# Building the expert gates of a routed layer: one-hot marks for 16 tokens in four products, and routing lookups merged over the heads

## The reference, cut to what matters

```python
q = (xb @ wq).reshape(PEER_BLOCK, PEER_HEADS, 2, PEER_HALF)
s = jnp.einsum('thpd,hpkd->thpk', q, sub_keys)             # 8 heads, 2 halves, 128 keys
s_top, i_top = lax.top_k(s, PEER_TOPK)                     # 16 of 128, twice
cand_s = s_top[:, :, 0, :, None] + s_top[:, :, 1, None, :] # pairs
cand_i = i_top[:, :, 0, :, None] * 128 + i_top[:, :, 1, None, :]
best_s, best_pos = lax.top_k(cand_s, PEER_TOPK)            # 16 of the pairs
experts = jnp.take_along_axis(cand_i, best_pos, axis=-1)
g = jax.nn.softmax(best_s, axis=-1)
act = gelu(einsum('thkd,td->thk', expert_u[experts], xb))
return einsum('thk,thkd->td', g * act, expert_v[experts])
```

## Time and profile before

| what | us |
|---|---|
| median of three runs | 2895.91 |
| profiled execution | 2900.16 |
| its span | 2898.3 |
| PE busy | 2657.9 (92%) |
| PEld busy | 2140.2 (74%) |
| DVE busy | 1856.9 (64%) |
| ACT busy | 949.5 (33%) |
| POOL busy | 1643.7 (57%) |

### The profile page before, as it was taken

How to read it: one execution, slowest core, us unless ns; L and a number is a source line. 1 busy time by engine, 2 the same in 40 slices (tenths; PEclk the granted TensorE clock), 3 DMA queues, 4 the chain that set the end, 5 groups by cost and what they waited for, 6 DMA issues and landing times.

```text
span 2898.3 us, 36976 instructions
## 1 busy us (share of the span) xinstructions
PE 2657.9 (92%) x13468; PEld 2140.2 (74%) x13468; DVE 1856.9 (64%) x3298; ACT 949.5 (33%) x1656; POOL 1643.7 (57%) x964
## 2 busy tenths in 40 slices
PE   7999999999899999999899999918777889999998
PEld 6888787678767788788677888816565667888886
DVE  6432398744664444200365079999999966888886
ACT  2001312833474101111242144314343444444443
POOL 4665457965403566646645557616455556666673
PEclk9999999999999999999999999959898999999998
DMA  4223122122342322322213245514454558888883
GB/s 157 87 87 121 58 88 94 31 66 77 110 146 109 116 92 112 109 88 101 98 41 111 92 175 217 217 44 182 170 217 200 217 217 306 290 289 289 289 289 131
DMA packets 139988, 429.93 MB, mean 148 GB/s; under 512 B 8800, under 2 KB 79584, under 8 KB 116704
## 3 DMA queue, kind: packets, MB, share of 16 engines
q1 hardware_dynamic: 125376, 353.40, 33.8%
q10 hardware_dynamic: 7200, 68.68, 6.1%
q0 software_dynamic: 7296, 6.31, 0.9%
HBM read 358.10 MB, written 73.40 MB: 149 GB/s over the span
## 4 chain that ended last, share of the span: by engine, by line
PE 64%; DVE 18%; issue 8%; POOL 6%; DMA 2%; ACT 1%; DVEq 1%; SPq 0%; ACTq 0%; POOLq 0%
PE bank L1144 8%; PE bank L1145 8%; DVE work L2316 6%; PE bank L697 4%; PE bank L698 4%; PE bank L700 4%; POOL rpb_tiles L2464 3%; PE bank L958 3%; PE bank L953 3%; PE bank L954 3%; PE bank L755 3%; PE bank L727 3%; PE bank L749 3%; PE bank L728 3%; PE bank L732 3%
## 5 line engine op out<-in xcount | busy, mean ns | idle before, releaser
L2502 POOL TENSOR_TENSOR expert_parts<-ring,expert_parts 128x1024 fp32r<-128x1024 f32 x256 | 696.3, 2722 | 495.4 <-ACT expert_parts L1586 492.7
L2526 POOL CAST w_parts<-ring 128x1024 fp32r<-128x1024 f32 (+3 forms) x212 | 228.8, 1079 | 636.3 <-DMA ring<-in_wstream 153.0
L2528 POOL TENSOR_TENSOR w_parts<-ring,w_parts 128x1024 fp32r<-128x1024 f32 (+3 forms) x212 | 512.1, 2416 | 17.0
L1586 ACT ACTIVATE expert_parts<-ring 128x1024 fp32r<-128x1024 f32 x256 | 271.2, 1060 | 538.5 <-PE bank L1145 531.0
L1144 PE MATMUL bank<-h_rounded,expert_parts 128*128 128x512 f32 x1024 | 414.0, 404 | 0.7 <-ACT work L1598 0.7
L1144 PE MATMUL bank<-weighted,expert_parts 128*128 128x512 f32 x1024 | 401.9, 393 | 9.9 <-DVE weighted L2348 9.9
L1145 PE MATMUL bank<-h_rest,expert_parts 128*128 128x512 f32 x1024 | 406.1, 397 | 0.0
L1145 PE MATMUL bank<-weighted,expert_parts 128*128 128x512 f32 x1024 | 401.5, 392 | 0.0
L2316 DVE SCALAR_TENSOR_TENSOR work<-const,trig,work 128x256 f16<-128x256 f32 x512 | 346.3, 748 | 0.0
L2348 DVE SCALAR_TENSOR_TENSOR weighted<-weighted,hF 128x512 fp32r<-128x512 f32 x128 | 309.5, 2419 | 51.3 <-ACT weighted L1666 48.1
L1144 PEld LDWEIGHTS bank<-weighted,expert_parts 128*128 128x128 f32 x1024 | 194.2, 190 | 51.2 <-issue 6.0
(11 more groups left out here) (430 smaller groups left out, 5155.4 us busy)
## 6 DMA issues: line engine op xcount, KB each, us to landing
ring<-in_wstream SPq DMA_DIRECT2D x128, 2048.0 KB, 7.8
hidden<-hF ACTq DMA_DIRECT2D x32, 1024.0 KB, 4.0
gates<-work ACTq DMA_DIRECT2D x16, 2048.0 KB, 10.7
hF<-hidden SPq DMA_DIRECT2D x32, 1024.0 KB, 9.5
work<-gates SPq DMA_DIRECT2D x32, 1024.0 KB, 12.8
rpb_tiles<-in_rpb POOLq DMA_DIRECT2D x192, 16.0 KB, 2.2
work<-rpb_tiles POOLq DMA_DIRECT2D x24, 128.0 KB, 5.4
ring<-in_wstream SPq DMA_DIRECT2D x5, 512.0 KB, 4.0
```

The costliest lines, as they stand in the source:

```text
L1586: act.activation(expert_chunk(j, 0), ring_chunk(p, j), ACT.Copy, scale=1.0 - 1.0 / SPREAD)\
L2502: nc.gpsimd.tensor_tensor(expert_chunk(j, 1), ring_chunk(p, j), expert_chunk(j, 0), ALU.subtract).then_inc(made, 1)
L2526: g.tensor_copy(parts[0], source).then_inc(hi, 1)
L2528: g.tensor_tensor(parts[1], source, parts[0], ALU.subtract).then_inc(made, 1)
```

## The change

- G_A and G_B are laid out with tokens innermost: G_A as [part, number, token], G_B as [number, token], 16 tokens adjacent. A new constant tile, G_RULER, holds each number 0 to 127 sixteen times.
- A batch of marks is four instructions of 2048 16-bit elements each, all operands 16-bit: compare with the first index, compare with the second index, multiply the first marks by the gate's high part, and (in place) by its low part. The first and the third are followed by a wait for their end. The 16 instructions L2316 and the one L2323 of a batch go.
- A product's operands are now every sixteenth 16-bit number of these tiles (a step of 32 bytes). Their number, shape and order stay.
- ScalarE's three copies of the banks, and `choice_moved` with TensorE's wait for it, go. VectorE waits for the transposes and reads banks 4 to 6 itself, with four instructions of 512 elements; G_RULER is made before that wait.
- In `routing`, the eight instructions L2265 of a quarter become one of 960 elements, and the eight L2291 of a half become one of 2048.

```diff
-        G_A = area(24576, 2, GC, N_KEYS).bitcast(f16).rearrange("p b t (l r) -> p b t l r", l=2)
-        G_B = area(28672, 2, GC, N_KEYS // 2).bitcast(f16)
+        G_A = area(24576, 2, 2 * N_KEYS * GC // 2).bitcast(f16).rearrange("p b (l r t) -> p b l r t", l=2, t=GC)
+        G_B = area(28672, 2, N_KEYS * GC // 2).bitcast(f16).rearrange("p b (r t) -> p b r t", t=GC)
+        G_RULER = area(30720, N_KEYS * GC // 2).bitcast(f16).rearrange("p (r t) -> p r t", t=GC)
...
-                                mm = pe.matmul(bank[:, 4 + b, t * P:(t + 1) * P], G_B[:, j // 2, 4 * b + t, :],
-                                               G_A[:, j // 2, 4 * b + t, l, :], start=(l == 0), stop=(l == 1))
+                                mm = pe.matmul(bank[:, 4 + b, t * P:(t + 1) * P], G_B[:, j // 2, :, 4 * b + t],
+                                               G_A[:, j // 2, l, :, 4 * b + t], start=(l == 0), stop=(l == 1))
...
-                pe.wait_ge(signal("choice_moved"), 3)
...
-                for c in range(3):
-                    act.wait_ge(signal("choice_turned"), c + 1)
-                    act.activation(E_T[c], bank[:, 4 + c, :], ACT.Copy).then_inc(signal("choice_moved"), 1)
...
-                    for h in range(PEER_HEADS):
-                        ins = v.tensor_tensor(
-                            R_CAND[:, h, 16:136].rearrange("p (i j) -> p i j", i=15),
-                            sv[:, h, 0, 1:16].rearrange("p (i a) -> p i a", a=1).broadcast_to([P, 15, 8]),
-                            sv[:, h, 1, 0:8].rearrange("p (a j) -> p a j", a=1).broadcast_to([P, 15, 8]), ALU.add)
+                    ins = v.tensor_tensor(
+                        R_CAND[:, :, 16:136].rearrange("p h (i j) -> p h i j", i=15),
+                        sv[:, :, 0, 1:16].rearrange("p h (i a) -> p h i a", a=1).broadcast_to([P, PEER_HEADS, 15, 8]),
+                        sv[:, :, 1, 0:8].rearrange("p h (a j) -> p h a j", a=1).broadcast_to([P, PEER_HEADS, 15, 8]),
+                        ALU.add)
...
-                        for h in range(PEER_HEADS):
-                            ins = v.tensor_tensor(R_EQ2[:, h * 16:(h + 1) * 16, :], R_EQ[:, h * 16:(h + 1) * 16, :],
-                                                  sif[:, h, s, :].rearrange("p (a j) -> p a j", a=1)
-                                                  .broadcast_to([P, 16, 16]), ALU.mult)
-                        order(ins)
+                        order(v.tensor_tensor(R_EQ2.rearrange("p (h k) j -> p h k j", h=PEER_HEADS),
+                                              R_EQ.rearrange("p (h k) j -> p h k j", h=PEER_HEADS),
+                                              sif[:, :, s, :].rearrange("p h (a j) -> p h a j", a=1)
+                                              .broadcast_to([P, PEER_HEADS, 16, 16]), ALU.mult))
...
+                    def of(x, n):
+                        return x[:, ds(n * GC, GC)].rearrange("p (a t) -> p a t", a=1).broadcast_to([P, N_KEYS, GC])
                     for b in range(2):
                         n = 2 * m + b
                         if not first(m):
                             dve.wait_ge(gated, 4 * n - 4)
-                        for t in range(GC):
-                            ins = v.scalar_tensor_tensor(
-                                out=G_A[:, b, t], in0=cst("iota").rearrange("p (l r) -> p l r", l=1)
-                                .broadcast_to([P, 2, N_KEYS]), scalar=E_T[0][:, ds(n * GC + t, 1)],
-                                in1=G_PARTS[:, :, ds(n * GC + t, 1)].broadcast_to([P, 2, N_KEYS]),
-                                op0=ALU.is_equal, op1=ALU.mult)
-                        ins.then_inc(first_hot, 1)
-                        e = G_SECOND[:, ds(n * GC, GC)].rearrange("p (t a) -> p t a", a=1)
-                        v.tensor_tensor(G_B[:, b], G_IOTA.rearrange("p (a r) -> p a r", a=1)
-                                        .broadcast_to([P, GC, N_KEYS]), e.broadcast_to([P, GC, N_KEYS]),
-                                        ALU.is_equal).then_inc(second_hot, 1)
-                dve.wait_ge(signal("choice_moved"), 3)
...
+                        order(v.tensor_tensor(G_A[:, b, 1], G_RULER, of(G_FIRST, n), ALU.is_equal))
+                        v.tensor_tensor(G_B[:, b], G_RULER, of(G_SECOND, n), ALU.is_equal).then_inc(second_hot, 1)
+                        order(v.tensor_tensor(G_A[:, b, 0], G_A[:, b, 1], of(G_HIGH, n), ALU.mult))
+                        v.tensor_tensor(G_A[:, b, 1], G_A[:, b, 1], of(G_LOW, n), ALU.mult).then_inc(first_hot, 1)
+                order(v.tensor_copy(G_RULER, cst("iota").rearrange("p (r a) -> p r a", a=1).broadcast_to([P, N_KEYS, GC])))
+                dve.wait_ge(signal("choice_turned"), 3)
+                v.tensor_copy(G_FIRST, bank[:, 4, :])
+                v.tensor_copy(G_SECOND, bank[:, 5, :])
+                order(v.tensor_scalar(G_HIGH, bank[:, 6, :], GATE_SCALE, None, ALU.mult))
+                order(v.scalar_tensor_tensor(out=G_LOW, in0=bank[:, 6, :], scalar=GATE_SCALE, in1=G_HIGH,
+                                             op0=ALU.mult, op1=ALU.subtract))
+                order.laps(S // GC // 2, body, 4)
```

More of the change, by code:

```diff
@@ L450, in build @@
         R_E = area(6656, NT, 3, P)
-        E_T = [trig.rearrange("p a t c -> p (a t c)"), rs[:, 0, :], rs[:, 1, :]]
         U_SLOTS = N_KEYS // 4
@@ L459, in build @@
         G_STAGE = area(0, 2, N_KEYS, GT)
-        G_A = area(24576, 2, GC, N_KEYS).bitcast(f16).rearrange("p b t (l r) -> p b t l r", l=2)
-        G_B = area(28672, 2, GC, N_KEYS // 2).bitcast(f16)
[L462 to L465, removed]
+        G_A = area(24576, 2, 2 * N_KEYS * GC // 2).bitcast(f16).rearrange("p b (l r t) -> p b l r t", l=2, t=GC)
+        G_B = area(28672, 2, N_KEYS * GC // 2).bitcast(f16).rearrange("p b (r t) -> p b r t", t=GC)
+        G_RULER = area(30720, N_KEYS * GC // 2).bitcast(f16).rearrange("p (r t) -> p r t", t=GC)
+        G_HIGH, G_LOW = (area(31744 + j * S // 2, S // 2).bitcast(f16) for j in range(2))
+        G_FIRST, G_SECOND = (rs[:, j, 0:S // 2].bitcast(f16) for j in range(2))
         GATE_SCALE = 32768.0
@@ L2321, in body @@
-                        ins.then_inc(first_hot, 1)
-                        e = G_SECOND[:, ds(n * GC, GC)].rearrange("p (t a) -> p t a", a=1)
-                        v.tensor_tensor(G_B[:, b], G_IOTA.rearrange("p (a r) -> p a r", a=1)
-                                        .broadcast_to([P, GC, N_KEYS]), e.broadcast_to([P, GC, N_KEYS]),
-                                        ALU.is_equal).then_inc(second_hot, 1)
-                dve.wait_ge(signal("choice_moved"), 3)
-                v.tensor_copy(G_IOTA, cst("iota"))
```

## The result

The changed kernel takes 2989.65 us (median of four, 2986.95 to 2993.4) against 2895.07 us before: a ratio of 1.0326, 95% interval 1.0309 to 1.0344. It is 95 us slower; the forecast was 94 us faster.

What follows compares the result with a forecast made beforehand. VectorE was taken to bound routing's end and the 16 gate slots. From the profiled 2900.2 us, gate slots -56 (408.2 to 352) and routing -38 gave 2806; the runs' median lies 4.3 lower: 2802 us, range 2745 to 2884.

Steps and rivals of the forecast that it cites:

- the price of the products' operands: Gate products on TensorE: stepped operands cost twice the dense price, 109 ns a product, group 1.74 us, slot 22.0 us.
- The slow rival: Gate products stop overlapping: 219 ns each, slot 29.0 us, gate stage +57 us, total 2915 us; chance 0.11.
- its point of decision: Gate stage: the slow outcome decides from 6.97 us for a row, that is from 200 ns for a product.
- Routing: Merged instructions on VectorE ahead of the choices save 38 us (29 to 56), multiply 31.6 with six stalls; on the path in full.
- The marks: VectorE's gate batch: four packed instructions at 1.22 us, at most 9.3 us with two stalls; VectorE leaves the path.
- ScalarE's copies and the ruler: Between routing and gates: dropping the copies, VectorE reading banks itself and making the ruler cost nothing.
- The first rival's bound: Gate slots: strided operands cost nothing, VectorE and GpSimd exclude each other for 19.4 us a slot; total 2760 us; chance 0.30.

Runs made afterwards that it cites:

- The run with halves: Changed kernel with 2 tokens innermost (4-byte step on both product operands), plus GpSimd's second part of a row made by two half-size instructions: 2748.5 us, ratio 0.947.
- the 4-byte step: Changed kernel with 2 tokens innermost in place of 16, so both operands of a gate product step by 4 bytes: 2765.54 us, ratio 0.9524.

## Why the prediction was wrong

**The step that failed is the price of the products' operands.** It was named as the number that "decides most" and was left to an inference: the weight loads depend on the width of a number (98 against 188 ns), so a stepped operand costs twice. The loads are the wrong operand. The moving one sets the price, at 219 ns by itself, and the cost goes with the 16-byte pieces touched, 1.75 to 1.79 ns each. With 229 instead of 109 ns the group is 3.66 instead of 1.74 us: 64 x 1.92 = 123 us on the gate stage. The next 41 us are, all but two, the granted clock, which nothing in the forecast had: it assumed full clock once TensorE stopped waiting. Together these are 164 of the 169 us between 352 and 521; the last 5 are rows of 3.84 where 3.76 had been reckoned.

The slow rival had the price almost right (219 ns) by luck, for its reason was wrong: products still overlap (423 ns long, 241 ns from start to start); they are slow because of what they read. Its 2915 us were 75 too few, for it too left out the clock and had the larger gain in routing. It was given 0.11 although the forecast itself said that no row showed such an operand; two ends as far apart as 54 and 317 ns, on the engine that was about to become the bound, called for a range that reached its point of decision, 200 ns.

**Routing was right in kind and too large.** 38 us were forecast, 22 came (62.8 to 40.7 us of waiting). The merged multiply met GpSimd eight times out of eight, not six, and the term left out the compare in front of it: L2288 before was stalled once in eight (median 2288), its counterpart in the changed kernel has a median of 4415 ns. GpSimd is now the one that waits during the long instruction (the one from 1802.84 above, under the compare), goes on as soon as that ends, and meets VectorE's next two-operand instruction (the multiply at 1804.16). 8 x (4.16 - 2.40) = 14 us of the missing 16 lie there, by the two means (33.3 and 19.2 us in all). Counted in the traces, merging removed stalls but fewer than reckoned: 24 instructions were stalled before (19 of L2291, where the forecast reckoned sixteen-odd, one L2288, four L2265), 16 after (all eight L2284, seven L2282, one L2258). The run with halves shows the mechanism.

**The marks were right, for the stage as it came out.** 1.22 us for a packed instruction, VectorE off the path, ScalarE's copies and the ruler without cost. They show their worth where the products are cheap: with the 4-byte step the gate stage is 298.3 us, 110 less than before, at a granted clock of 1.00.

**The first rival's bound was too pessimistic.** With 1.22 and 2.40 us, 19.4 us of a slot were added up as mutual exclusion; the 4-byte step ran 18.6 with VectorE busy for 271 of 298 us. In that trace the instructions of the two engines overlap a little at each hand-over, so the sum of their undisturbed durations is no lower bound.

## What to carry to other kernels

A layout that suits the engine that writes a tile is paid for by the engine that reads it. Before a packed layout is put under a matrix product, count the 16-byte pieces that the moving operand touches: a step of two 16-bit numbers (4 bytes) cost next to nothing here, and beyond that each piece cost 1.75 to 1.79 ns. The innermost group need only be as long as packing asks for, two numbers here, not as long as the batch.

An instruction that waits for another engine's running instruction is made faster by shortening that one (4.36 to 3.26 us here). Merging many short instructions into one removed stalls from it here (19 to 8) and handed some to the line in front (1 to 7).

## What the runs showed of the hardware

- The price of a 128x128x128 product of 16-bit numbers with both operands stepped: 57, 112, 224 and 229 ns for steps of 4, 8, 16 and 32 bytes, 54 dense. With the moving operand alone stepped by 32 bytes 219, with the weights alone 64. Whether the same holds for four-byte numbers was not tried.
- TensorE's granted clock fell to 1.2 GHz in stretches of the gate stage with the 16- and 32-byte steps of the moving operand although the trace shows no idle time of TensorE there (510.9 of 510.9 us busy at 0.93 with 16 bytes, 521.0 of 521.0 at 0.92 with 32); with 8 and 4 bytes it stayed at 1.00. What it did before the fall shown above was a group of slow gate products (2157.08 to 2160.75); the group before that (from 2149.58) was followed by a row at full clock. Without these falls, the gate stage of the changed kernel would have been about 40 us shorter. What decides which group is followed by a fall stays open.
